# A hybrid GLA and short-convolution layer: the mixer's scan taken two chunks at a time, its conv gate copied to SBUF, block 2's input asked for earlier, the mixer norms' sums in the bank ring

## What is computed

```
h = rmsnorm(x)*(1+m1)+m0;  x = x + 0.5*m2 * (silu(h@w1)*(h@w3))@w2        # first FFN, d_ff 2816
h = rmsnorm(x)*(1+m4)+m3;  x = x + m5 * (concat[o_gla, o_conv] @ w_out)    # mixer
h = rmsnorm(x)*(1+m7)+m6;  x = x + 0.5*m8 * swiglu(h)                      # second FFN
y = rmsnorm(x)
```

```
S_t = diag(alpha_t) S_{t-1} + k_t^T v_t ;  o_t = q_t S_t      # forwards and backwards, 4 heads of 64 x 128
o_gla  = rmsnorm_per_head(o_f + o_b) * gla_norm * silu(g)
o_conv = cb * conv3(cc * ch)                                  # width-3 conv along the tokens
```

## Time and profile before

| | us |
|---|---|
| three runs | 1280.44, 1469.43, 1278.35; median 1280.44 |
| the profiled execution | 1285.47 |
| its span on core 1, the slowest | 1283.9 |
| spans of the other cores | 1274.2 to 1282.8 |
| PE busy on core 1 | 1232.8 (96%) |
| DVE, ACT, POOL busy | 592.7, 388.3, 177.8 |
| mean granted clock of PE, core 1 | 0.982 |

### The profile page before, as it was taken

The page is one execution under the profiler, slowest core; times in us unless marked ns, Lnnn a source line. Parts: engine busy times, 40 slices in busy tenths (PEclk is TensorE's granted clock), DMA queues, the critical chain, the costliest instruction groups (busy, mean ns, idle before and its releaser), DMA issues.

```text
span 1283.9 us, 18529 instructions; the slowest of 8 cores (1274.2 to 1283.9 us)
## 1 busy us (share of the span) xinstructions
PE 1232.8 (96%) x6248; PEld 560.5 (44%) x6248; DVE 592.7 (46%) x944; ACT 388.3 (30%) x638; POOL 177.8 (14%) x282
## 2 busy tenths in 40 slices
PE   3899999999999999999999999999999999999996
PEld 0344444444444444444444444444444444444444
DVE  3233158255562355866577766311242122432566
ACT  5244100111001335677444445411101111001353
POOL 3112000100001000523344413201001000000000
PEclk9899999999999999999999999899999999999998
DMA  9994735757437110021414226605204221030113
GB/s 207 170 233 97 117 100 168 127 149 210 101 98 118 66 66 1 2 33 30 72 30 114 45 77 100 99 1 93 40 1 66 33 34 33 1 50 1 66 66 132
DMA packets 38684, 104.12 MB, mean 81 GB/s; under 512 B 4416, under 2 KB 11072, under 8 KB 36416
## 3 DMA queue, kind: packets, MB, share of 16 engines
q0 software_dynamic: 19008, 53.72, 25.4%
q1 hardware_dynamic: 19584, 49.23, 11.8%
HBM read 137.76 MB, written 14.68 MB: 119 GB/s over the span
## 4 chain that ended last, share of the span: by engine, by line
PE 89%; DVE 4%; DMA 3%; issue 2%; ACT 1%; POOL 1%; DVEq 0%; ACTq 0%; POOLq 0%
PE ps L240 89%; DMA sb_arena<-w_ada 3%; DVE sb_arena L268 2%; DVE sb_arena L257 1%; ACT sb_arena L253 1%; POOL sb_arena L237 1%; DVE sb_arena L872 0%; PE ps L244 0%; POOL sb_arena L264 0%; DVEq L141 0%; ACT L253 0%; POOL sb_arena L262 0%; DVEq L1341 0%; ACTq L141 0%; DVE sb_modT L257 0%
## 5 line engine op out<-in xcount | busy, mean ns | idle before, releaser
L240 PE MATMUL ps<-sb_arena 128*128 128x512 bf16 (+5 forms) x5840 | 1187.8, 367 | 18.2 <-ACT sb_arena L253 7.5
L240 PEld LDWEIGHTS ps<-sb_arena 128*128 128x128 bf16 (+3 forms) x5840 | 536.0, 98 | 664.7 <-issue 90.2
L253 ACT ACTIVATE sb_arena<-ps 128x512 f32<-128x512 f32 (+3 forms) x281 | 166.1, 599 | 681.3 <-PE ps L240 612.9
L257 DVE TENSOR_TENSOR sb_arena<-sb_arena,ps 128x512 bf16<-128x512 f32 (+1 forms) x208 | 142.9, 687 | 432.6 <-PE ps L240 388.1
L268 DVE SCALAR_TENSOR_TENSOR sb_arena<-ps,sb_der,sb_arena 128x512 f32<-128x512 f32 (+1 forms) x200 | 145.1, 728 | 110.9 <-PE ps L240 110.9
L253 ACT ACTIVATE sb_arena<-sb_arena 128x512 f32<-128x512 f32 (+3 forms) x194 | 124.2, 661 | 88.4 <-DVE sb_arena L268 72.2
L237 POOL DMA_DIRECT2D sb_arena<-w_ffn x88 | 47.0, 545 | 596.3 <-PE ps L240 445.6
L257 DVE TENSOR_TENSOR sb_arena<-sb_arena 128x512 f32<-128x512 f32 (+1 forms) x126 | 83.2, 695 | 43.2 <-ACT sb_arena L253 42.5
L264 POOL TENSOR_SCALAR sb_arena<-sb_arena,sb_der,sb_modT 128x512 bf16<-128x512 f32 x48 | 50.7, 1059 | 245.8 <-DVE sb_arena L257 225.3
L268 DVE SCALAR_TENSOR_TENSOR sb_arena<-sb_arena,sb_vec 128x512 f32<-128x512 f32 (+1 forms) x72 | 53.2, 759 | 12.5 <-POOL sb_arena L262 7.6
L640 DVE SCALAR_TENSOR_TENSOR sb_arena<-sb_arena 128x1024 f32<-128x1024 f32 x48 | 58.4, 1216 | 0.0
(11 more groups left out here) (46 smaller groups left out, 155.1 us busy)
## 6 DMA issues: line engine op xcount, KB each, us to landing
sb_arena<-w_adaT SPq DMA_DIRECT2D x48, 512.0 KB, 3.6
sb_arena<-w_ffn POOLq DMA_DIRECT2D x44, 512.0 KB, 9.4
sb_arena<-w_ffn POOLq DMA_DIRECT2D x44, 256.0 KB, 10.7
sb_arena<-w_ada POOLq DMA_DIRECT2D x12, 512.0 KB, 33.0
y<-sb_arena SPq DMA_DIRECT2D x24, 256.0 KB, 2.4
sb_arena<-x POOLq DMA_DIRECT2D x4, 1024.0 KB, 11.8
sb_arena<-x SPq DMA_DIRECT2D x4, 1024.0 KB, 16.8
xspill<-sb_arena SPq DMA_DIRECT2D x4, 1024.0 KB, 3.9
```

Of the source, the lines that this page charges most:

```text
L240: return P.add("pe", lambda e: e.matmul(out, lhsT, rhs, start=start, stop=stop), reads=flat(reads), writes=flat(writes))
L253: return P.add("act", lambda e: e.activation(out=out, in_=in_, func=func, **kw), reads=flat(reads), writes=flat(writes))
L257: return P.add(eng, lambda e: e.tensor_tensor(out=out, in0=in0, in1=in1, op=op), reads=flat(reads), writes=flat(writes))
```

## The change

1. `core(p)` goes two chunks at a time: the scores of the next two, the state parts of these two, their local parts, then the masks of the next two. Two calls of `filler` stand ahead of each pair, and one half of `onorm_b` (one head) behind each call. The rates in `core(1)` are 1.0 and not 1.3, so more units of the output projection come after it.
2. In part 2 of `conv_unit` ACT copies the gate from PSUM to SBUF, and the last product of `taps` reads the copy.
3. Block 2's x waits for pair 1's second panel, and the slices of its norm are taken 4, 4, 4, 2 in place of 4, 3, 4, 3.
4. The column sums of the norms in `phase_a` go to a bank of the ring.
5. The third panel of `w_out` is asked for at part 0 of the last conv row, not at its part 2.

```diff
@@ norm_slices
+                if k0 == 0:
+                    st["b"] = rbank() if nrm["ring"] else 7
-                    mm(ps[:, 7, :], onesB[:], bf(SQ + kc * KB, 512), kc == 0, kc == last, ...
+                    mm(ps[:, st["b"], :], onesB[:], bf(SQ + kc * KB, 512), kc == 0, kc == last, ...
@@ start
-        load_x(2, [F1.pair[2][1][1]], "sp")
+        load_x(2, [F1.pair[1][1][1]], "sp")
-            tick((0, 0, 0, 4, 3, 4, 3, 0)[i])
+            tick((0, 0, 0, 4, 4, 4, 2, 0)[i])
@@ conv_unit
+            gate = f32(O_CT + 2 * CVB, 512)
+            if part == 2:
+                t_gate = P.alloc("cgate", O_CT + 2 * CVB, 2 * KB)
+                act(gate, ps[:, b, :], AF.Copy, [t_ps[b]], [t_gate])
...
-                tt("dve", bf(cm_off(j, blk), 512), cu, ps[:, b, :], ALU.mult, [t_cu, t_ps[b]], [t_cm[(j, blk)]])
+                tt("dve", bf(cm_off(j, blk), 512), cu, gate, ALU.mult, [t_cu, t_gate], [t_cm[(j, blk)]])
+            if (part, j, blk) == (0, 3, NB - 1):
+                load_wo(2)
@@ core: the loop
-            scores(0)
-            for c in range(16):
-                filler(rates[c // 4], keep if c < 13 else min(keep, 5))
-                while deferred and deferred[0][0] <= c:
-                    onorm_b(*deferred.pop(0)[1])
-                if c + 1 < 16:
-                    scores(c + 1)
-                pv_state(c)
-                pv_local(c)
-                if c % 4 == 3:
-                    deferred.append((c + 1, onorm_a(c // 4)))
+            for c in range(2):
+                scores(c)
+            for c in range(2):
+                mask(c)
+            held = None
+            for c in range(0, 16, 2):
+                for hh in range(2):
+                    filler(rates[c // 4], keep if c < 14 else min(keep, 5))
+                    if held:
+                        onorm_b(*held, hh)
+                held = None
+                if c < 14:
+                    scores(c + 2)
+                    scores(c + 3)
+                pv_state(c)
+                pv_state(c + 1)
+                pv_local(c)
+                pv_local(c + 1)
+                if c < 14:
+                    mask(c + 2)
+                    mask(c + 3)
+                if c % 4 == 2:
+                    held = onorm_a(c // 4)
```

More of the change, by code:

```diff
@@ L325, in later @@
             bg.extend((blk, f) for f in slices)
-        nrm = {"n": 0, "t": 0, "wide": True}
+        nrm = {"n": 0, "t": 0, "wide": True, "ring": False}
         adds = []
@@ L901, in build_program @@
         wgA = []
+        nrm["ring"] = True
         for blk in range(NB):
@@ L907, in build_program @@
                 wgA = [load_at("wg%d" % i, SQ + i * 2 * KB, 2 * KB, wg_d[i], 1024) for i in range(4)]
+        nrm["ring"] = False
         CVR = [120 * KB + i * 2 * KB for i in range(4)] + [152 * KB + i * 2 * KB for i in range(4)]
@@ L1129, in scores, with mask @@
                            [t_k[p][blk], t_q[p][blk]], [t_ps[b]])
+            def mask(c):
+                o = (c % 2) * 256
                 tt("dve", atv(c).rearrange("p (h f) -> p h f", f=256), ps[:, 4:6, o:o + 256],
@@ L1138, in pv_state @@
                         mm(ps[:, 6 + hh, cc * 128:(cc + 1) * 128], xpv(dr, c)[hh * 64:(hh + 1) * 64, :],
-                           qview(p, dr, blk)[hh * 64:(hh + 1) * 64, cc * 128:(cc + 1) * 128], dr == 0, False,
+                           qview(p, dr, blk)[hh * 64:(hh + 1) * 64, cc * 128:(cc + 1) * 128], dr == 0 and c % 2 == 0, False,
                            [t_xp[(dr, c)], t_q[p][blk]], [t_ps[6 + hh]])
@@ L1147, in pv_local @@
                         mm(ps[:, 6 + hh, cc * 128:(cc + 1) * 128], vv, atv(c)[:, hh * 256 + dr * 128:hh * 256 + (dr + 1) * 128],
-                           False, dr == 1, [t_vt[c], t_at[c % 2]], [t_ps[6 + hh]])
+                           False, dr == 1 and c % 2 == 1, [t_vt[c], t_at[c % 2]], [t_ps[6 + hh]])
             def onorm_a(blk):
@@ L1162, in onorm_a @@
                 return blk, st
-            def onorm_b(blk, st):
-                bs = []
-                for hh in range(2):
[L1167 to L1183, removed]
@@ L1185, in core, with onorm_b @@
-            scores(0)
-            for c in range(16):
-                filler(rates[c // 4], keep if c < 13 else min(keep, 5))
-                while deferred and deferred[0][0] <= c:
-                    onorm_b(*deferred.pop(0)[1])
-                if c + 1 < 16:
-                    scores(c + 1)
+            def onorm_b(blk, st, hh):
+                b = rbank()
+                mm(ps[:, b, :], onesB[:], st[hh][2], True, True, [t_ones, st[hh][3]], [t_ps[b]])
+                r = f32(O_RS + hh * 2 * KB, 512)
+                t_r = P.alloc("rs%d" % hh, O_RS + hh * 2 * KB, 2 * KB)
+                act(r, ps[:, b, :], AF.Ln, [t_ps[b]], [t_r], scale=1.0 / 128, bias=EPS)
+                act(r, r, AF.Exp, [t_r], [t_r], scale=-0.5)
+                hg = p * 2 + hh
+                t_s = t_sg[(hg, blk)]
+                tt("dve" if p == 1 and blk == 3 else "pool", sgv(hg, blk), st[hh][0], r, ALU.mult, [st[hh][1], t_r], [t_s])
+                t_mix[(hg, blk)] = t_s
@@ L1194, in core @@
                 pv_local(c)
-                if c % 4 == 3:
-                    deferred.append((c + 1, onorm_a(c // 4)))
-            return deferred, onorm_b
+                pv_local(c + 1)
[4 more added lines that the diff above has]
+                    held = onorm_a(c // 4)
+            return held, onorm_b
         filler(2.0)
@@ L1206, in build_program @@
         dfr, ob = core(0, [1.25, 1.25, 1.25, 1.25])
-        chain_first = []
         filler(1.0)
-        for _, a in dfr:
-            ob(*a)
+        for hh in range(2):
+            ob(*dfr, hh)
         chain(1, 1.0)
-        dfr, ob = core(1, [1.3, 1.3, 1.3, 1.3])
+        dfr, ob = core(1, [1.0, 1.0, 1.0, 1.0])
         assert len(fill) <= 8, len(fill)
```

6 lines of the change are left out of this document (2 added, 4 removed).

## The result

| | before | changed |
|---|---|---|
| runs, us | 1280.44, 1469.43, 1278.35, 1397.73 | 1266.98, 1264.46, 1267.98, 1265.92 |
| median | 1280.44 (of the three known ahead) | 1266.45 |
| profiled execution | 1285.47 | 1266.98 |
| spans of the cores | 1274.2 to 1283.9 | 1259.9 to 1265.3 |

The ratio is 0.9898 with a 95% interval of 0.987 to 0.9926: the change gains 1.0%, about 13 us. That is clear of noise, and less than the 2% that the prediction named as what a measurement can tell from no change. (All ratios here leave out the executions, two of before's four, in which a die ran at a lower clock.) 1265 was forecast, in a range of 1257 to 1276. The sum was close by luck: its largest term, the waits of the scans, came to 3.5 us in place of 7.7, the clock of the second scan to 0 in place of 1.7, and the start to 4.9 in place of 1.5, so that the errors mostly cancelled.

The account below looks back on a forecast made before the run. PE was taken as full in the first FFN, with 17.9 us of the two scans not work. Terms 3.0 + 7.7 + 1.5 + 1.6 + 1.7 = 15.5 us off 1285.5 give 1270.0; the median is 5 lower: 1265, range 1257 to 1276.

Parts of the forecast that it names:

- waits of the scans: Both scans: of 9.7 us that PE waits for banks, masks and column sums, 7.7 go; bounds 0 and 9.7.
- clock of the second scan: Second scan's end: PE's lower clock for 3.4 us behind two waits goes, 1.7 us back; bounds 0 and 1.7.
- start: First FFN: PE's 2.05 us wait for POOL's h tiles shrinks, perhaps the low clock too; 1.5 us, bounds 0.5 and 4.
- switches: Both scans: 16 fewer changes between full and half array rows, about 0.19 us for each in and out; 3.0 us.
- projections: Ahead of the k projection: PE's wait for bank 7 goes with a ring bank; 1.6 us, bounds 0 and 1.6.
- copies, rates, `w_out`: Gate copies on ACT, lower filler rates in `core(1)` and the earlier `w_out` panel: each costed at nothing.
- Rival C: Scans: POOL and DVE stretch each other more, masks come late, 5.2 us lost again; 1270 us, chance 0.13.
- Rival B: Scans: waits only move, PE waiting once for two masks; 1 or 2 us of waits go; 1273 us, chance 0.18.
- E: Scans: slower, DVE becomes the bound, needing 147 us against PE's 117; 1295 us, chance 0.05.
- D: Scan waits, start and stretches at clock 0.81: more goes than counted, 13.2 us more; 1252 us, chance 0.04.

Follow-up runs that it names:

- the scan without waits: First scan of the changed kernel with ACT's scaling one unit later and both halves of `onorm_b` behind the second filler: 44.7 us; ratio 0.987, median 1261.28 us.
- the bank 7 run: Changed kernel with the mixer norms' column sums in bank 7 again: ratio 0.989, projections 67.2 us on every core.
- the last one: Changed kernel with ACT's scaling one unit later and both halves of `onorm_b` behind the second filler, but without the gate copy: ratio 0.9977, first scan 52.6 us.

## What held of the prediction, and which step failed

| term | forecast | measured | from |
|---|---|---|---|
| switches | 3.0 | 3.0 | inferred: 1.7 us for 9 groups, in the scan without waits |
| waits of the scans | 7.7 | 3.5 | below |
| half clock of the second scan | 1.7 | 0 | still there, just behind it, on 7 of 8 cores |
| start | 1.5 | 4.9 (2.9 on core 1) | FFN stretch |
| projections | 1.6 | 1.4 | both profiles and the bank 7 run |
| copies, rates, `w_out` | 0 | 0 | |
| sum | 15.5 | 12.8 | the ratio gives 13 |

**The waits were mis-sized, and that is the step that failed.** "I leave 2 us of waits and take 7.7": 3.5 us went. By the same working the changed kernel has 46.1 - 43.0 - 1.7 = 1.4 us in the first scan and, with 134 large matmuls, 42.6 - 36.1 - 1.7 = 4.8 in the second. 6.2 of 9.7 stayed, and 5.23 of them are the four waits of 1.13, 1.33, 0.43 and 2.34 in the rows. What was wrong in the working is the sentence on ACT: "Queued behind it on ACT are the conv copies and the chain's scalings, which PE needs a unit later at the soonest". I looked for what the copy would delay, and not for what stood behind `make_u`'s scaling, which already waited for DVE. The squares, Ln and Exp do stand there; the two kernels with the scaling later and with the norm later each took 1.13 us away there, by two unlike edits. I had gone through DVE's order and not through ACT's.

**Rival C was real, in my forecast's place.** The Trainium skill's "GPSIMD Engine Reference" ("Specifications") has POOL and a DVE instruction with two SBUF inputs contend. The traces agree: 946 against 691 ns with and without POOL's products, and 683 in both for the masks, which read PSUM. I had priced it at 5.2 us by masks pushed late. Its effect reached PE through ACT's order instead, and in the run without POOL's products the cure cost more than it gave.

**The start was too small.** I took one POOL operation sooner by 0.7 and part of a clock. Two things were missed. Six of the eight cores waited 0.40 to 1.87 us for x through ACT's squares, which I dismissed because PE on core 1 did not. On core 4 before, ACT and PE:

```profile
77.76 2.19 ACT L253 ACTIVATE sb_arena<-sb_arena 128x512 bf16<-128x512 f32 x4 [2.44 <-DMA sb_arena<-x]
```

```profile
78.53 1.94 PE L240 MATMUL ps<-sb_arena,sb_onesB 128*128 128x512 bf16 x4 [1.15 <-ACT sb_arena L253]
```

Even on core 1 ACT stood 1.28 for it. The ends of the stretch hinted at this: six cores reached the seventh group within 1.1 us (139.5 to 140.6) after starts from 55.4 to 59.1. And the last h alone on POOL took 0.77 us, where in a pair beside DVE's multiplies it took 2.34/2 = 1.17, so the wait shrank from 2.05 to 0.75 and the half clock behind it, on all eight cores before, was on none after.

**The clock** of the second scan did not come back. It is at its lower level for 3.4 us from about 722 on seven cores, behind the wait of 2.34; core 5, with the same wait, kept the full clock. The wait alone does not decide it: in the three runs that leave the mixer as it is, all cores have a wait of 2.34 or 2.35 there, and the lower level came on 5, 6 and 2 of the 8. What does decide it was not settled.

**The slowest core** fell by 18.6 us in the two profiles, more than the medians by 5. That is before's core 1: it had four stretches of 15 us at 0.81, from 442, 751, 795 and 820 us, worth 2.9 each; in the changed profile core 1 has two of about 5 us, worth 1 each. Core 5, with a mean clock of 0.989 before and 0.990 after, fell from 1274.2 to 1263.2. What starts and ends these stretches was not settled.

Rival B (waits only move) described the measured scans better than the forecast: it left 1.4 us for waits that go, against 3.5 measured and 7.7 forecast, and its time of 1273 was missed because the start gave 3.4 us more than either had. E did not show: DVE was busy 30.4 of 46.1 and 34.9 of 42.6 us. D's condition, no stretch at 0.81, was met in the eleven profiles ahead of the last one, and the best ratio among them is 0.987 against D's 0.978 (1252 by 1280.4). (In E, 14 POOL products at 1.6 us are 22.4 and not 21; nothing hangs on it.)

Of the prediction's own signs these came true: 9 groups in a scan, no wait ahead of the k projection, 0.75 at the FFN's wait, and x asked for at 57.71. These did not: few waits over 0.3 us, scans of 43 to 45 us for the same work (46.1 for the first), and a clock of 1.00 at the second scan's end. C's sign, gate products over 0.8 us, did come.

## What to carry to other kernels

When a wait is taken from a queue that runs in order, read what stands behind the next waiting instruction on every engine, also on the ones that were not edited: here ACT, about half busy in the scans (23.55 of 46.1 us), carried DVE's delay to PE. The worth of an edit depends on what stands beside it: the gate copy gained nothing without the pairing, 0.9 us with it, and 12.6 us (9.2 without the half clocks) after ACT's order was mended. So undo one part from the best version too before it is dropped. And where cores with unlike starts reach a place at nearly one time, look for what they all wait for, also on the cores that the profile doesn't show first.

## What was not expected of the hardware

A DVE product with two SBUF inputs of 128 x 512 f32 took 0.69 us alone and up to 1.78 with a POOL product beside it, while the POOL product kept its 1.26:

```profile
706.18 1.78 DVE L257 TENSOR_TENSOR sb_arena<-sb_arena 128x512 bf16<-128x512 f32 x1 [0.17 <-DVE sb_arena L268]
```

```profile
706.15 1.26 POOL L257 TENSOR_TENSOR sb_arena<-sb_arena 128x512 bf16<-128x512 f32 x1 [0.69 <-ACT sb_arena L253]
```

POOL began 0.03 us sooner, and DVE ended 0.55 us behind POOL's end: it seems to have stood until POOL was through. Had the two shared at half speed, DVE's 0.69 would have become some 1.4 (an estimate), and POOL's operation would have grown too. The Trainium skill's "SBUF — State Buffer", section "SBUF: two separate sides", calls the shared pair an exclusive lock that the one who starts first holds for its whole instruction; these two rows agree with it.
